# Memory heads of a two-block layer: the query and key weights multiplied into one matrix per head, and scores taken against the convolved rows

## The chip, the cores and the metric

The kernel runs on 1 core of one Trainium2 chip. The time is device microseconds of one execution. The kernel before takes 653.73 us, the median of 3 runs (653.63 to 653.75).

## The reference, cut to what matters

The program is two transformer blocks in a row on 256 rows of 1024 values, all in float32. The second block's mixer has eight attention heads and four memory heads (an mLSTM in chunks of 64, which the kernel computes over the whole 256 x 256 triangle). The memory heads take the rows `x_m`, convolve them over four positions, and form a query, a key and a value per head with 128 x 128 weights:

```
xc  = silu(_causal_conv(x_m, conv_w, conv_b))          # 256 x 512, four heads of 128
mq  = einsum('bshd,hde->bhse', xch, w_mq)
mk  = einsum('bshd,hde->bhse', xch, w_mk) * (128 ** -0.5)
mv  = einsum('bshd,hde->bhse', xmh, w_mv)
qk  = einsum('bhtd,bhsd->bhts', q_, k_) * w_intra       # scores, weighed by gates
...
ml_out = (hm + ml_skip * xc) * silu(z)
x = x + concatenate([attn_out, ml_out]) @ w_o
```

The key is used for nothing but the scores in this form. `xc` is used a second time, for the skip. After the mixer comes a mixture of experts (32 experts, two per row), whose weights (48 chunks of 2 MB) are read once, and a last gated projection.

## The kernel before, in words

Every engine has one instruction stream written out by hand, and counted semaphores order them. A semaphore's name with `_done` is raised by PE, one with `_ready` or `_high` mostly by ACT or DVE. Large products are split in a rounded and a remaining part (`product`, lines 2020 to 2022, three matmuls each).

The first block ends with `hand_over` on ACT (lines 771 to 794), which normalises the rows of each half of 128; PE meanwhile keeps busy with matmuls on zeros (`keep_busy`, L1996) and turns the rows with `turn_h` (L2015). Then, in the second mixer, PE makes in this order: the compressed projections (L2299), `x_m` and `z` (`tiles`), attention queries, keys and values (`product`), and then the stretch that the change touches. There `gate(0, ...)` makes the memory query (8 matmuls, L2397, of 256 columns, banks 2 and 3), three of six groups of attention scores come (L2413, with a mask matmul L2415), `gate(1, ...)` makes the memory key (8 more at L2397), three more groups of scores follow, two groups of transposed scores (L2459), and then a mix that is written out: `qk(h)` (the memory scores, L2432 and L2433, all in bank 6), `mix_values` (the memory values, L2467), `num(h)` (L2443 to L2445, all in bank 2), further transposed scores and `attend`. After them stand the products with `w_o`, without a break in PE's stream.

DVE in that stretch finds the maximum of each of the six score groups (L1651), then makes `round_wo(4)`, `round_wo(5)`, `weigh(0)`, `round_wo(6)`, `round_wo(7)`, `weigh(1)`, `divide(0)`, `weigh(2)` and so on. A `round_wo(n)` (L1660) copies an eighth of `w_o` (128 x 1024) to its rounded part, from SBUF to SBUF. A `weigh(h)` (L1667) multiplies the scores in bank 6 by the gates and so frees the bank for `qk(h + 1)`. A `divide(h)` frees bank 2 for `num(h + 1)`.

ACT copies the queries and keys out of PSUM (L1028 and L1053), makes the exponentials of the scores (L1040) and of the gates (L1046), and copies the values (L1060).

POOL makes `lower_wo(n)`, n = 0 to 7 (L712): the rest of each eighth of `w_o`, the raw weight less its rounded part, 128 x 1024, both inputs in SBUF. Its order is `lower_wo` 0 to 3, then a wait for `mk_done`, then the skip's two multiplications of `xcT` in place (L718, L720), then a wait until all eight parts are rounded, `lower_wo` 4 and 5, a multiplication of `szT` (L724), and `lower_wo` 6 and 7. Parts 0 to 3 are rounded by ACT early, 4 to 7 by DVE as above.

The DMA queue (SP) loads the weights in a fixed order. For the second mixer it issues `x_m`'s weights, `z`'s, `w_uq`, `w_ukv`, `w_mq`, `w_mk` and `w_mv` (L555 to L561), `w_o`'s halves, and then the experts' chunks into a ring of 12 places (`load_chunk`, L565). The first 12 are issued as places come free in the mixer; each later one waits until PE has used the chunk 12 before it. PE's loop over the experts holds a chunk until the last round of its group of four experts.

Of the kernel before, what the change touches and what calls it, by code (L numbers as in the profile page):

```python
# [22 lines left out]
P = 128  # L23
SEQ = 256
# [22 lines left out]
M_HEADS = 4  # L47
# [9 lines left out]
UNIT = 4096  # L57
# [12 lines left out]
def build(nc, a, out):  # L70
    with ExitStack() as ctx:
# [8 lines left out]
            "pe_mix2": (("c_done", 2), ("xm_done", 2), ("cT_done", 2), ("turned_done", 1), ("z2_done", 1),  # L80
                        ("gT_done", 1), ("negM_done", 1), ("z2_late", 1), ("negM_late", 1), ("qa_done", 4), ("ka_done", 4), ("v2_done", 2),
                        ("mq_done", 2), ("sa_done", 3), ("mk_done", 2), ("sa_late", 3), ("mv_done", 2)),
# [5 lines left out]
            "act_mix2": (("cs_ready", 1), ("cstd_ready", 1), ("gln_ready", 1), ("xm_ready", 2), ("ct_high", 1), ("lat_high", 3), ("sz_ready", 2),  # L88
                         ("xc_ready", 2), ("qn_ready", 2), ("xc_late", 2), ("qn_late", 2), ("kn_ready", 4), ("v2_ready", 2), ("mq_ready", 2),
                         ("floor_ready", 1), ("raw_ready", 3), ("wexp_ready", 1), ("mk_ready", 2), ("raw_late", 3), ("wexp_late", 3),  # L90
# [9 lines left out]
            "landed_root2": (("q1_landed", 16), ("wm_landed", 48)),  # L100
# [186 lines left out]
        mkT = v3(take(1024), 4)  # L287
# [153 lines left out]
        wm = W[:, 3 * UNIT:3 * UNIT + 1536].rearrange("p (m h e) -> p m h e", m=3, h=M_HEADS)  # L441
# [49 lines left out]
        def _(sp):  # L491
# [45 lines left out]
            sp.wait_ge(sig("x_ready"), 2)  # L537
            for dst, src in ((wr[:, :, 0:N_GRP], a["w_router_group_2"][0].rearrange("(k p) n -> p k n", p=P)),
                             (wr[:, :, N_GRP:36], a["w_router_expert_2"][0].rearrange("(k p) n -> p k n", p=P)),
                             (brt[:, 0:N_GRP], a["b_router_group_2"][0:1, :].broadcast_to([P, N_GRP])),  # L540
                             (brt[:, N_GRP:36], a["b_router_expert_2"][0:1, :].broadcast_to([P, N_EXP])),
                             (bif[:, 0:4], a["b_igate_2"][0:1, :].broadcast_to([P, M_HEADS])),
                             (bif[:, 4:8], a["b_fgate_2"][0:1, :].broadcast_to([P, M_HEADS])),
                             (pos.bitcast(I32), a["pos_tok"]),
                             (ptok, a["p_2"][0, 0].rearrange("(b p) c -> p b c", p=P))):
                sp.dma_start(dst, src).then_inc(sig("small_landed"), 16)
# [12 lines left out]
            sp.dma_start(wm[:, 0], a["w_mq_2"][0].rearrange("h d e -> d h e")).then_inc(sig("wm_landed"), 16)  # L559
            sp.dma_start(wm[:, 1], a["w_mk_2"][0].rearrange("h d e -> d h e")).then_inc(sig("wm_landed"), 16)  # L560
            sp.dma_start(wm[:, 2], a["w_mv_2"][0].rearrange("h d e -> d h e")).then_inc(sig("wm_landed"), 16)  # L561
# [68 lines left out]
        def _(pool):  # L630
# [84 lines left out]
            for n in range(4):  # L715
                lower_wo(n)
            pool.wait_ge(sig("mk_done"), at("mk_done", 2))
# [3 lines left out]
            pool.wait_ge(sig("dense_high"), 32 + 8 + 8)  # L721
            lower_wo(4)
            lower_wo(5)
# [24 lines left out]
        def _(act):  # L748
# [22 lines left out]
            def hand_over(r, b):  # L771

                n = 2 * r + b
                for h in range(2):
                    if h == 0:
                        act.wait_ge(sig("y_done"), n + 1)
                    else:
                        act.wait_ge(sig("yg_ready"), 2 * n + 1)
                    act.activation(junk[:, 512 * h:512 * h + 512], ps[:, 4 + 2 * b + h, :], ACT.Square, scale=D ** -0.5,
                                   accum_out=stat[:, 60 + h:61 + h]).then_inc(sig("ysq_ready"), 1)  # L780
                act.wait_ge(sig("yms_ready"), n + 1)
                act.wait_ge(sig("ysq_ready"), 2 * n + 2)
# [268 lines left out]
            for h in range(2):  # L1051
                act.wait_ge(sig("mk_done"), at("mk_done", h + 1))
                act.mul(mkT[:, 2 * h:2 * h + 2, :], v3(ps[:, 2 + h, :], 2), float(P) ** -0.5).then_inc(sig("mk_ready"), 1)  # L1053
# [937 lines left out]
        def _(pe):  # L1991
# [300 lines left out]
            keep_busy(0, 3)  # L2292
            turn_h(2, 0)
            keep_busy(3, 1)
            for b in range(TB):
                for k in range(KD):
                    if k % 4 == 0:
                        pe.wait_ge(sig("hT_ready"), 4 * 2 + 2 * b + k // 4 + 1)
                    last = pe.matmul(ps[:, 2 + b, 0:424], hT[:, k, b * P:(b + 1) * P], wA[:, k, :],  # L2299
                                     start=(k == 0), stop=(k == KD - 1))  # L2300
                    if b == 0 and k >= 6:
                        turn_h(2, 1, (k - 6,))
                last.then_inc(sig("c_done"), 1)
# [83 lines left out]
            pe.wait_ge(sig("wm_landed"), at("wm_landed", 48))  # L2387

            def gate(m, banks, name, free):

                for n in range(2):
                    for f in free[n]:
                        pe.wait_ge(sig(f[0]), at(*f))
                    pe.wait_ge(sig(("xc_ready", "xc_late")[n]), at(("xc_ready", "xc_late")[n], 2))
                    for i in range(2):
                        h = 2 * n + i
                        last = pe.matmul(ps[:, banks[n], 256 * i:256 * i + 256], wm[:, m, h, :], xcT[:, h, :], start=True, stop=True)  # L2397
                    last.then_inc(sig(name), 1)

            gate(0, (2, 3), "mq_done", ((("qn_late", 1), ("qr_late", 1)), (("qn_late", 2), ("qr_late", 2))))  # L2400
# [18 lines left out]
            for n in range(3):  # L2419
                scores(n)  # L2420
            gate(1, (2, 3), "mk_done", ((("mq_ready", 1),), (("mq_ready", 2),)))
            for n in range(3, 6):
                scores(n)

            def qk(h):

                if h == 0:
                    pe.wait_ge(sig("mq_ready"), at("mq_ready", 2))
                    pe.wait_ge(sig("mk_ready"), at("mk_ready", 2))
                else:  # L2430
# [16 lines left out]
            def turned_scores(n):  # L2447

                kb, h, heads = ST[n]
                o = v3(ps[:, ST_BANK[n], :], heads)  # L2450
                if n < 2:
                    pe.wait_ge(sig("mk_ready"), at("mk_ready", 2))
                elif n < 4:
                    pe.wait_ge(sig("raw_late"), at("raw_late", n))
                else:
                    pe.wait_ge(sig("e_ready"), at("e_ready", n - 3))
                for hh in range(heads):
                    for b in range(kb, TB):
                        last = pe.transpose(o[:, hh, (b - kb) * P:(b - kb + 1) * P], raw_block(b, h + hh, kb), ident[:])  # L2459
                last.then_inc(sig("st_done"), 1)  # L2460

            def mix_values():

                pe.wait_ge(sig("raw_late"), at("raw_late", 1))
                for b in range(TB):
                    for h in range(M_HEADS):
                        last = pe.matmul(ps[:, 4 + b, h * P:(h + 1) * P], xmT[:, h, 3 + b * P:3 + (b + 1) * P], wm[:, 2, h, :],  # L2467
                                         start=True, stop=True)
                    last.then_inc(sig("mv_done"), 1)
# [335 lines left out]
        "conv_ffn", "w_down", "p_2", "w_in_2", "w_ukv_2", "w_mq_2", "w_mk_2", "w_mv_2",  # L2805
# [39 lines left out]
```

## Time and profile before

| what | value |
|---|---|
| median of 3 runs | 653.73 us |
| the profiled execution, its own time | 653.55 us |
| its span | 651.8 us |
| granted clock, mean | 0.983 |
| PE / PEld busy | 616.8 us (95%) / 472.7 us (73%) |
| DVE / ACT / POOL busy | 378.9 us (58%) / 284.3 us (44%) / 47.7 us (7%) |
| read from HBM | 173.17 MB, 267 GB/s over the span |
| DMA traffic, 480 to 600 us | 423 to 432 GB/s |

Busy shares are means over stages with different limits. What counts for an edit is which wait ends last in its own stage. The stages that matter here are the second mixer (from 308 to 402 us), the routing (402 to 421.6 us), the experts (421.6 to 628 us) and the tail. Times within the span count from its start.

### The profile page before, as it was taken

How to read it: one execution, taken by the hardware profiler on the slowest of the kernel's cores; microseconds unless marked ns; L12 is line 12 of the kernel's file. 1: busy time of each engine (PE TensorE's matmuls, PEld its weight loads, DVE VectorE, ACT ScalarE, POOL GpSimd, SP SyncE). 2: the span in 40 equal slices, each digit the busy share in tenths (PEclk: the TensorE clock that was granted, in tenths of full speed). 3: DMA queues.
4: the chain of work that ended last, by engine and by line, in shares of the span. 5: the costliest groups of instructions: out<-in, count | busy, mean ns of one | idle time of the engine just before them, and what ended most of it. 6: DMA issues, size and time to landing. Idle time of an engine off the chain costs nothing. (4 is left out here: it accounts for less than half of the span.)

```text
span 651.8 us, 11050 instructions
## 1 busy us (share of the span) xinstructions
PE 616.8 (95%) x4314; PEld 472.7 (73%) x4318; DVE 378.9 (58%) x671; ACT 284.3 (44%) x454; POOL 47.7 (7%) x75
## 2 busy tenths in 40 slices
PE   8999999999999999999999999899999976769895
PEld 5999998899999999998699798644444431325365
DVE  5596868578777767766889475632222321103286
ACT  6773376575555555456794831610011000000184
POOL 3000000300000000001010860000000000000010
PEclk9999999999999999999999999999999997889998
DMA  8943543767755555500943698999899999999931
GB/s 328 371 161 130 179 130 113 272 190 257 233 189 177 179 177 176 187 3 2 379 153 130 259 350 309 429 426 427 343 427 430 426 423 429 429 425 425 424 165 66
DMA packets 52957, 174.82 MB, mean 268 GB/s; under 512 B 4790, under 2 KB 29490, under 8 KB 45874
## 3 DMA queue, kind: packets, MB, share of 16 engines
q1 hardware_dynamic: 52240, 172.54, 68.7%
q10 hardware_dynamic: 674, 1.69, 0.7%
q8 instruction: 30, 0.49, 0.3%
q14 instruction: 13, 0.11, 0.0%
HBM read 173.17 MB, written 1.05 MB: 267 GB/s over the span
## 5 line engine op out<-in xcount | busy, mean ns | idle before, releaser
L2020 PE MATMUL ps<-hT_high,w_up_parts 128*128 128x256 f32 x320 | 90.8, 284 | 0.0
L2022 PE MATMUL ps<-hT_high,w_up_parts 128*128 128x256 f32 x320 | 90.5, 283 | 0.0
L2021 PE MATMUL ps<-hT_low,w_up_parts 128*128 128x256 f32 x320 | 90.5, 283 | 0.0
L1423 DVE TENSOR_TENSOR w_up_parts<-W,w_up_parts 128x1024 fp32r<-128x1024 f32 x44 | 52.2, 1222 | 22.2 <-ACT w_up_parts L884 22.2
L2020 PEld LDWEIGHTS ps<-hT_high,w_up_parts 128*128 128x128 f32 x320 | 61.4, 192 | 0.5
L2021 PEld LDWEIGHTS ps<-hT_low,w_up_parts 128*128 128x128 f32 x320 | 61.4, 192 | 0.4
L2022 PEld LDWEIGHTS ps<-hT_high,w_up_parts 128*128 128x128 f32 x320 | 61.4, 192 | 0.0
L1104 ACT ACTIVATE sg<-ps 128x256 f32<-128x256 f32 x9 | 3.5, 384 | 123.0 <-PE ps L2633 123.0
L2633 PE MATMUL ps<-W,junk 128*32 128x512 f32 x368 | 45.7, 622 | 8.2 <-DMA W<-in_w_moe_dram 8.1
L884 ACT CAST w_up_parts<-W 128x1024 fp32r<-128x1024 f32 x44 | 44.5, 1048 | 20.3 <-PE ps L2022 19.0
L2020 PE MATMUL ps<-h_high,dense_high 128*128 128x256 f32 x160 | 45.8, 286 | 0.1
L2021 PE MATMUL ps<-h_low,dense_high 128*128 128x256 f32 x160 | 45.3, 283 | 0.0
L2022 PE MATMUL ps<-h_high,dense_low 128*128 128x256 f32 x160 | 45.3, 283 | 0.0
L1446 DVE SCALAR_TENSOR_TENSOR arena<-ps,arena 128x255 f32<-128x255 f32 x80 | 33.1, 476 | 17.2 <-ACT arena L920 16.9
L2617 PEld LDWEIGHTS ps<-arena,x_tok 128*128 128x128 f32 x288 | 32.8, 192 | 8.3 <-issue 6.7
L1297 DVE TENSOR_TENSOR dense_low<-W,dense_high 128x1024 fp32r<-128x1024 f32 x31 | 36.1, 1219 | 2.7 <-ACT dense_high L813 2.6
L2617 PE MATMUL ps<-arena,x_tok 128*128 128x128 f32 x288 | 34.4, 278 | 1.2 <-DVE arena L1878 1.2
L813 ACT CAST dense_high<-W 128x1024 fp32r<-128x1024 f32 x30 | 29.4, 1045 | 12.9 <-PE ps L2022 10.0
L2633 PEld LDWEIGHTS ps<-W,junk 128*32 128x32 f32 x368 | 10.5, 111 | 32.4 <-issue 19.8
L1871 DVE SCALAR_TENSOR_TENSOR sg<-sg,stat,ps 128x256 f32<-128x256 f32 x9 | 4.3, 481 | 48.1 <-ACT sg L1104 48.1
L2020 PE MATMUL ps<-w_down_high,uact_high 128*128 128x512 f32 x80 | 31.4, 392 | 0.1
L2020 PEld LDWEIGHTS ps<-h_high,dense_high 128*128 128x128 f32 x160 | 30.7, 192 | 1.0 <-issue 0.7
(500 smaller groups left out, 1386.5 us busy)
## 6 DMA issues: line engine op xcount, KB each, us to landing
W<-in_w_moe_dram SPq DMA_DIRECT2D x22, 2048.0 KB, 21.3
arena<-in_w_moe_dram SPq DMA_DIRECT2D x14, 2048.0 KB, 30.3
W<-in_w_up_dram SPq DMA_DIRECT2D x22, 1024.0 KB, 7.8
W<-in_w_in_dram SPq DMA_DIRECT2D x7, 2048.0 KB, 10.5
W<-in_w_down_dram SPq DMA_DIRECT2D x11, 1024.0 KB, 5.0
spare<-in_w_moe_dram SPq DMA_DIRECT2D x4, 2048.0 KB, 15.9
hh<-in_w_moe_dram SPq DMA_DIRECT2D x4, 2048.0 KB, 33.3
W<-in_w_out_dram SPq DMA_DIRECT2D x2, 2048.0 KB, 9.1
```

The source lines that it names most:

```text
L813: act.copy(piece(panel_hl(n)[0], n, c), piece(panel(n), n, c)).then_inc(sig("dense_high"), 1)
L884: act.copy(w_up_hl[0][:, c], U[q][:, :, g, i * P:(i + 1) * P]).then_inc(sig("up_high"), 1)
L1104: act.activation(sg, ps[:, 2, 0:F_EXP], ACT.Silu).then_inc(sig("sg_ready"), 1)
L1297: dve.tensor_tensor(piece(panel_hl(n)[1], n, c), piece(panel(n), n, c), piece(panel_hl(n)[0], n, c).bitcast(F32), ALU.subtract).then_inc(s ...
L1423: dve.tensor_tensor(w_up_hl[1][:, c], U[q][:, :, g, i * P:(i + 1) * P], w_up_hl[0][:, c].bitcast(F32), ALU.subtract).then_inc(sig("up_low" ...
L1446: dve.scalar_tensor_tensor(o, s, w, o, ALU.mult, ALU.add).then_inc(sig("tap_done"), 1)
L1871: dve.scalar_tensor_tensor(sg, sg, gslot, ps[:, 2, F_EXP:2 * F_EXP], ALU.mult, ALU.mult).then_inc(sig("a_ready"), 1)
L2020: pe.matmul(o, lhs[0], rhs[0], start=first, stop=False, skip_group_check=True)
L2021: pe.matmul(o, lhs[0], rhs[1], start=False, stop=False, skip_group_check=True)
L2022: return pe.matmul(o, lhs[1], rhs[0], start=False, stop=last_k, skip_group_check=True)
L2617: last = pe.matmul(ps[:, h, (k % 4) * P:(k % 4 + 1) * P], x_tok[:, b, k * P:(k + 1) * P], hot[:, b, :], start=(b == 0), stop=(b == 1))
L2633: last = pe.matmul(ps[CAP * c:CAP * c + CAP, 2, :], xg[:, k, CAP * c:CAP * c + CAP], up_chunk(CPG * g + j)[:, c, kk, :], start=(k == 0), s ...
```

## The change

In the hand-over between the blocks, PE multiplies each head's query weight by its key weight: `am[h] = w_mq[h] @ w_mk[h].T`, scaled by ACT. The former `gate(0)` uses `am` where it used `w_mq`; `gate(1)`, the key's copies on ACT and `mkT` go, and `qk` takes `xcT` where it took `mkT`. The two weights come in one transfer (512 KB, laid out by the host as transposes), issued early in the first block's MLP, in front of the small ones. Since `xcT` is now read by all four `qk`, POOL multiplies it in place only after the last of them, and makes `lower_wo` 4 and 5 ahead of that, each as soon as its own part is rounded.

```diff
 # SP
             sp.wait_ge(sig("x_ready"), 2)
+            sp.dma_start(wqk, a["w_mqk"]).then_inc(sig("wqk_landed"), 16)
             for dst, src in ((wr[:, :, 0:N_GRP], a["w_router_group_2"][0].rearrange("(k p) n -> p k n", p=P)),
...
-            sp.dma_start(wm[:, 0], a["w_mq_2"][0].rearrange("h d e -> d h e")).then_inc(sig("wm_landed"), 16)
-            sp.dma_start(wm[:, 1], a["w_mk_2"][0].rearrange("h d e -> d h e")).then_inc(sig("wm_landed"), 16)
-            sp.dma_start(wm[:, 2], a["w_mv_2"][0].rearrange("h d e -> d h e")).then_inc(sig("wm_landed"), 16)
+            sp.dma_start(wmv, a["w_mv_2"][0].rearrange("h d e -> d h e")).then_inc(sig("wm_landed"), 16)
 # POOL
-            for n in range(4):
+            for n in range(6):
                 lower_wo(n)
-            pool.wait_ge(sig("mk_done"), at("mk_done", 2))
+            pool.wait_ge(sig("qk_done"), 4)
             pool.tensor_tensor(xcT[:], xcT[:], szT[:], ALU.mult).then_inc(sig("gates_folded"), 1)
...
-            pool.wait_ge(sig("dense_high"), 32 + 8 + 8)
-            lower_wo(4)
-            lower_wo(5)
             pool.tensor_tensor(szT[:], szT[:], ...)
 # ACT, in hand_over, behind the two squares
+                if n == 3:
+                    act.wait_ge(sig("am_done"), at("am_done", 1))
+                    act.mul(am, v3(ps[:, 3, :], M_HEADS), float(P) ** -0.5).then_inc(sig("am_ready"), 1)
                 act.wait_ge(sig("yms_ready"), n + 1)
 # ACT, in the second mixer
             exp_gate(0)
-            for h in range(2):
-                act.wait_ge(sig("mk_done"), at("mk_done", h + 1))
-                act.mul(mkT[:, 2 * h:2 * h + 2, :], v3(ps[:, 2 + h, :], 2), float(P) ** -0.5).then_inc(sig("mk_ready"), 1)
 # PE, behind the first block
-            keep_busy(0, 3)
+            pe.wait_ge(sig("wqk_landed"), at("wqk_landed", 16))
+            for h in range(M_HEADS):
+                last = pe.matmul(ps[:, 3, h * P:(h + 1) * P], wqk[:, 0, h, :], wqk[:, 1, h, :], start=True, stop=True)
+            last.then_inc(sig("am_done"), 1)
             turn_h(2, 0)
-            keep_busy(3, 1)
+            keep_busy(2, 1)
...
+                    if b == 1 and k == 0:
+                        pe.wait_ge(sig("am_ready"), at("am_ready", 1))
 # PE, second mixer
-            for n in range(3):
-                scores(n)
-            gate(1, (2, 3), "mk_done", ((("mq_ready", 1),), (("mq_ready", 2),)))
-            for n in range(3, 6):
+            for n in range(6):
                 scores(n)
...
-                    pe.wait_ge(sig("mk_ready"), at("mk_ready", 2))
...
-                pe.matmul(ps[:, 6, 0:256], mkT[:, h, 0:P], mqT[:, h, :], start=True, stop=True)
-                pe.matmul(ps[:, 6, 256:384], mkT[:, h, P:SEQ], mqT[:, h, P:SEQ], start=True, stop=True).then_inc(sig("qk_done"), 1)
+                pe.matmul(ps[:, 6, 0:256], xcT[:, h, 0:P], mqT[:, h, :], start=True, stop=True)
+                pe.matmul(ps[:, 6, 256:384], xcT[:, h, P:SEQ], mqT[:, h, P:SEQ], start=True, stop=True).then_inc(sig("qk_done"), 1)
 # PE, turned_scores(n), n < 2
-                    pe.wait_ge(sig("mk_ready"), at("mk_ready", 2))
+                    pe.wait_ge(sig("raw_ready"), at("raw_ready", 2 + n))
```

## Rows read from the trace of the kernel before

**Rows 1.** The chain of waits that ended last: start us, us, what
```profile
421.59 0.54 issue
...
502.77 42.01 DMA W<-in_w_moe_dram
```

**Rows 2.** Busy time by engine in a stretch, around 460 us (stretch, its length, busy us and instructions, clock, DMA share, GB/s)
```profile
460.00:462.00 2.00, 2.00 (x22) 0.93 (x24) 1.39 (x3) 0.00 (x0) 0.00 (x0) 1.00 0.50 213
```

**Rows 3.** The DMA queue's issues in order of time
```profile
462.49 0.33 SPq L565 DMA_DIRECT2D W<-in_w_moe_dram  x1
```

**Rows 4.** Busy time by engine in a stretch of the second mixer
```profile
388.00:402.00 14.00, 14.00 (x71) 11.57 (x70) 10.78 (x33) 2.62 (x5) 0.32 (x1) 1.00 0.82 302
```

**Rows 5.** PE in order of time (start us, us, line, operation, count, idle before)
```profile
366.36 1.99 PE L2397 MATMUL ps<-arena,W 128*128 128x256 f32 x8
...
368.19 1.05 PE L2413 MATMUL ps<-arena 128*128 128x128 f32 x8
...
373.40 1.95 PE L2467 MATMUL ps<-W,arena 128*128 128x128 f32 x16
...
375.24 0.70 PE L2432 MATMUL ps<-arena 128*128 128x256 f32 x2
...
377.54 0.60 PE L2432 MATMUL ps<-arena 128*128 128x256 f32 x2
...
380.66 0.46 PE L2443 MATMUL ps<-arena,junk 128*128 128x129 f32 x2
```

**Rows 6.** ACT in order of time
```profile
310.95 0.29 ACT L783 ACTIVATE stat<-stat 128x1 f32<-128x1 f32 x1 [0.77 <-DVE stat L1247]
...
368.74 1.13 ACT L1053 ACTIVATE arena<-ps 128x512 f32<-128x512 f32 x2
...
370.21 1.14 ACT L1040 ACTIVATE W<-ps,arena 128x128 f32<-128x128 f32 x4 [0.34 <-DVE arena L1651]
```

**Rows 7.** ACT, DVE and PE early in the first block's MLP
```profile
143.58 3.90 ACT L884 CAST w_up_parts<-W 128x1024 fp32r<-128x1024 f32 x4 [0.97 <-DMA W<-in_w_up_dram]
...
158.27 0.69 DVE L1465 TENSOR_TENSOR uact_low<-arena,uact_high 128x512 fp32r<-128x512 f32 x1 [0.76 <-ACT uact_high L931]
...
160.87 0.40 PE L2020 MATMUL ps<-w_down_high,uact_high 128*128 128x512 f32 x1
```

**Rows 8.** POOL in order of time
```profile
369.02 2.35 POOL L718 TENSOR_TENSOR arena<-arena 128x1024 f32<-128x1024 f32 x1
...
371.45 1.89 POOL L720 TENSOR_TENSOR arena<-arena,par 128x1024 f32<-128x1024 f32 x1
...
376.69 2.36 POOL L712 TENSOR_TENSOR wo_low<-W,wo_high 128x1024 fp32r<-128x1024 f32 x1 [3.35 <-DVE wo_high L1660]
```

**Rows 9.** DVE in order of time, reductions, rounding copies and the weighing of scores
```profile
371.92 0.69 DVE L1651 TENSOR_REDUCE arena<-ps 128x2 f32<-128x512 f32 x1 [0.53 <-PE ps L2415]
...
372.65 1.24 DVE L1660 CAST wo_high<-W 128x1024 fp32r<-128x1024 f32 x1
...
375.10 0.69 DVE L1660 CAST wo_high<-W 128x1024 fp32r<-128x1024 f32 x1
...
375.10 1.51 DVE L1660 CAST wo_high<-W 128x1024 fp32r<-128x1024 f32 x2
...
376.52 0.55 DVE L1667 TENSOR_TENSOR junk<-ps,arena 128x384 f32<-128x384 f32 x1
```

**Rows 10.** POOL and DVE around 340 us
```profile
337.84 3.23 POOL L702 COPY arena<-arena 64x1792 f32<-64x1792 f32 x1 [28.96 <-DVE arena L1590]
...
338.32 1.20 DVE L1577 TENSOR_TENSOR z_low<-W,proj_high 128x1024 fp32r<-128x1024 f32 x1
...
339.45 2.15 DVE L1594 TENSOR_TENSOR_SCAN arena<-arena 4x256 f32<-4x256 f32 x1
...
342.09 0.68 DVE L1596 TENSOR_TENSOR_SCAN arena<-arena 4x256 f32<-4x256 f32 x1
```

**Rows 11.** DVE, its first instruction that needs the folded gates
```profile
397.23 0.69 DVE L1740 TENSOR_TENSOR hh<-ps,arena 128x512 f32<-128x512 f32 x1 [1.56 <-PE ps L2520]
```

More of the change, by code:

```diff
@@ L79, in build @@
                         ("o_done", 2), ("go_done", 2), ("onT_done", 2), ("u_done", 3), ("u_turned", 1)),
-            "pe_mix2": (("c_done", 2), ("xm_done", 2), ("cT_done", 2), ("turned_done", 1), ("z2_done", 1),
+            "pe_mix2": (("am_done", 1), ("c_done", 2), ("xm_done", 2), ("cT_done", 2), ("turned_done", 1), ("z2_done", 1),
                         ("gT_done", 1), ("negM_done", 1), ("z2_late", 1), ("negM_late", 1), ("qa_done", 4), ("ka_done", 4), ("v2_done", 2),
-                        ("mq_done", 2), ("sa_done", 3), ("mk_done", 2), ("sa_late", 3), ("mv_done", 2)),
+                        ("mq_done", 2), ("sa_done", 3), ("sa_late", 3), ("mv_done", 2)),
             "pe_route": (("oT_done", 2), ("hmT_done", 2), ("pT_done", 1), ("y2_done", 1), ("y2_half", 1), ("y2_late", 1), ("logits_done", 2), ("rank_done", 1),
@@ L87, in build @@
                          ("osq_ready", 1), ("ostd_ready", 1), ("sgo_ready", 2), ("uc_ready", 3)),
-            "act_mix2": (("cs_ready", 1), ("cstd_ready", 1), ("gln_ready", 1), ("xm_ready", 2), ("ct_high", 1), ("lat_high", 3), ("sz_ready", 2),
+            "act_mix2": (("am_ready", 1), ("cs_ready", 1), ("cstd_ready", 1), ("gln_ready", 1), ("xm_ready", 2), ("ct_high", 1), ("lat_high", 3), ("sz_ready", 2),
                          ("xc_ready", 2), ("qn_ready", 2), ("xc_late", 2), ("qn_late", 2), ("kn_ready", 4), ("v2_ready", 2), ("mq_ready", 2),
-                         ("floor_ready", 1), ("raw_ready", 3), ("wexp_ready", 1), ("mk_ready", 2), ("raw_late", 3), ("wexp_late", 3),
+                         ("floor_ready", 1), ("raw_ready", 3), ("wexp_ready", 1), ("raw_late", 3), ("wexp_late", 3),
                          ("mv_ready", 2), ("e_ready", 6), ("pT_ready", 1)),
@@ L99, in build @@
             "landed_root": (("q0_landed", 16), ("uq_landed", 32)),
-            "landed_root2": (("q1_landed", 16), ("wm_landed", 48)),
+            "landed_root2": (("q1_landed", 16), ("wqk_landed", 16), ("wm_landed", 16)),
             "pool_root": (("q_low", 1), ("krope_spread", 1)),
@@ L286, in build @@
         xmT = v3(take(4 * 259), 4)
-        mkT = v3(take(1024), 4)
+        off[0] += 512
+        am = v3(take(512), M_HEADS)
         vext = take(2 * 4 * 129).rearrange("p (b h e) -> p b h e", b=2, h=4)
@@ L439, in latent_piece @@
             return [t[:, :, 512 * j:512 * j + 512] for t in (uq, uq_hl[0], uq_hl[1])]
-        wm = W[:, 3 * UNIT:3 * UNIT + 1536].rearrange("p (m h e) -> p m h e", m=3, h=M_HEADS)
+        wmv = v3(W[:, 3 * UNIT + 1024:3 * UNIT + 1536], M_HEADS)
+        wqk = v4(spare[:, 0:1024], 2, M_HEADS)
         w_moe = a["w_moe"]
@@ L2386, in _ @@
                         [t.rearrange("p (h c) -> p h c", h=A_HEADS)[:, :, NOPE:P] for t in ukv_hl], True, True).then_inc(sig("v2_done"), 1)
[L2387 to L2400, printed above, removed]
+            for n in range(2):
+                pe.wait_ge(sig("qn_late"), at("qn_late", n + 1))
+                pe.wait_ge(sig("qr_late"), at("qr_late", n + 1))
+                pe.wait_ge(sig(("xc_ready", "xc_late")[n]), at(("xc_ready", "xc_late")[n], 2))
+                for i in range(2):
+                    h = 2 * n + i
+                    last = pe.matmul(ps[:, 2 + n, 256 * i:256 * i + 256], am[:, h, :], xcT[:, h, :], start=True, stop=True)
+                last.then_inc(sig("mq_done"), 1)
             pe.wait_ge(sig("v2_done"), at("v2_done", 2))
@@ L2466, in mix_values @@
                     for h in range(M_HEADS):
-                        last = pe.matmul(ps[:, 4 + b, h * P:(h + 1) * P], xmT[:, h, 3 + b * P:3 + (b + 1) * P], wm[:, 2, h, :],
+                        last = pe.matmul(ps[:, 4 + b, h * P:(h + 1) * P], xmT[:, h, 3 + b * P:3 + (b + 1) * P], wmv[:, h, :],
                                          start=True, stop=True)
@@ L2804 @@
 _INS = ["x", "norm_mix_post", "norm_ffn_post", "w_in", "gate_up_fwd", "gate_up_bwd", "w_out", "w_up",
-        "conv_ffn", "w_down", "p_2", "w_in_2", "w_ukv_2", "w_mq_2", "w_mk_2", "w_mv_2",
+        "conv_ffn", "w_down", "p_2", "w_in_2", "w_ukv_2", "w_mv_2",
         "b_igate_2", "b_fgate_2", "w_o_2", "w_router_group_2", "b_router_group_2", "w_router_expert_2",
@@ L2834 @@
     laid_out["w_q"] = _np.asarray(inputs["w_in"])[0][:, C_Q:C_Q + 512].reshape(KD, P, 4, P).transpose(1, 2, 0, 3).reshape(P, UNIT)
+    laid_out["w_mqk"] = _np.stack([_np.asarray(inputs[name])[0].transpose(2, 0, 1) for name in ("w_mq_2", "w_mk_2")], axis=1)
     laid_out["w_gate"] = _np.asarray(inputs["w_ple_gate_2"])[0].reshape(KD, P, 2, 512).transpose(2, 1, 0, 3)
```

## The prediction

> **What bounds the kernel now.** I read the chain that ended last first. From 502.77 us it runs on DMA: an expert chunk is issued when PE frees its place and lands 42.01 us later, behind all the others in the queue [rows 1]. Before that the chain is PE's own, back to 421.59 us, where PE enters the loop over the experts. Next I read the windows around 460 us, to see whether the DMA engines or PE set the moment at which that backlog begins. They do not move anything for half of the stretch from 460 to 462 us (share 0.50) [rows 2], because the queue's next issue stands at 462.49 us, behind a chunk that PE holds through the second round of its group [rows 3]. So DMA has run dry for about 1.5 us, and it starts again a fixed distance behind PE's start at 421.59. Whatever moves that start moves the end by the same amount, up to about 1.5 us of slack the other way if only DMA were early; since the earlier loads hang on the same PE steps, they move along.
>
> What sets 421.59? The windows of the second mixer show PE busy for all 14.00 us from 388 to 402 [rows 4], and the rows ahead of it follow each other without a gap: the key's matmuls run from 366.36 for 1.99 us, and the next score has begun at 368.19 [rows 5]. PE's stream has no cover there: an instruction taken out of it, or a wait put into it, counts in full, unless another engine is late next.
>
> **What is taken out.** The memory key's eight matmuls start at 366.36 and the next score starts at 368.19 [rows 5]: 8 instructions, 1.83 us. ACT loses two copies of PSUM, 1.13 us together [rows 6]. That one is worth nothing by itself, because right behind it ACT waited 0.34 us for DVE's maximum of group 3, which hangs on PE's scores [rows 6]; all of that moves with PE. With nothing else the sum is -1.83 us.
>
> **What is put in, and costs nothing or nearly.** Four 128-column matmuls stand where three on zeros stood, in a stretch where PE only waits for the normalised rows. By `mix_values`, sixteen of the same shape in 1.95 us [rows 5], they take 0.12 each, 0.49 together; the price is between 0 (the zeros took as long) and 0.5; I take 0. ACT's scaling of `am` is one 128 x 512 copy out of PSUM, 0.57 us by the pair at L1053 [rows 6]. It falls where ACT stood idle for 0.77 us before L783 [rows 6]: hidden with 0.2 us to spare; without that cover it would cost up to 0.6. The third new wait (`am_ready`, at PE's second compressed projection) comes microseconds after the copy. `qk` has the same shapes with `xcT` as with `mkT`: 0. The transposed scores now wait for `raw_ready`, which ACT reaches before 368.74 (its next rows [rows 6]), while PE gets there only behind the last maximum's scores, which end just ahead of 371.92 - 1.83 = 370.1 [rows 9]: 0.
>
> The 512 KB transfer goes into the queue early in the first MLP, ahead of eight small ones and of the loads of `w_up`. Those are exposed a little: ACT waited 0.97 us for one at 143.58 [rows 7]. 512 KB at 427 GB/s (the middle of the table's 423 to 432) are 1.2 us. ACT's and DVE's chain then reaches `uact_low` at 158.96 + 1.2 = 160.2 us instead of 158.96 (the row at 158.27, 0.69 long), and PE asks for it at 160.87 [rows 7]: hidden, with 0.7 us left. Bounds: 0, and up to 1.7 us if the queue takes 3.6 us over it. `w_mq` and `w_mk` leaving the later queue helps nobody who waits: 0.
>
> **What is moved: POOL.** This is where I see the change give back its gain. Before, DVE's four rounding copies run at 372.65 and after. POOL's subtractions of the same parts, L712, begin at 376.69, behind the last copy [rows 8]: the two never overlap. Only the first copy meets POOL, which works on L720 until 371.45 + 1.89 = 373.34 [rows 8]. That copy takes 1.24 us, while the one at 375.10 takes 0.69 with POOL idle [rows 9]. 1.24 is exactly 0.69 (from 372.65 to 373.34) plus 0.55. So either DVE stood still until POOL was through, or it ran at nearly half speed throughout. The scan at 339.45 decides for standing still, as far as one row can: 2.15 us against 0.68 for the same shape at 342.09, and it ends at 341.60, which is 0.53 behind the end of POOL's copy (337.84 + 3.23 = 341.07) [rows 10]. The maxima, which read PSUM, are not touched (0.69 for the maximum at 371.92, beside POOL's L720) [rows 8, 9].
>
> The Trainium skill says the same more sharply: "SBUF — State Buffer", section "Who interferes with whom", gives DVE and GpSimd one shared pair of ports, which whoever issues first holds for its whole instruction, and names copies and casts within SBUF among the DVE instructions that need it. By that rule the sum below is +0.8 to +1.3 us; by a mere slowing of the copies it is -1.1.
>
> After the change POOL makes `lower_wo(4)` as soon as copy 4 is done, and `lower_wo(5)` as soon as copy 5 is, right among DVE's copies 5, 6 and 7. Step by step, with DVE's last maximum at 371.92 - 1.83 = 370.09 and the copy 0.73 behind it as now [rows 9]:
> - copy 4: 370.82 to 371.51 (POOL idle). POOL starts 0.08 later, at 371.59 (now it starts at 376.69, and the two copies from 375.10 end 1.51 later, at 376.61), and takes 2.36 [rows 8, 9]: to 373.95.
> - copy 5 is stopped until 373.95 and ends 0.55 later, 374.50. `weigh(0)` to 375.0. PE has been ready for `qk(1)` since 375.24 - 1.83 = 373.41 [rows 5] and waits 1.6 us.
> - POOL's second subtraction runs from 374.58 to 376.94. Copy 6 is stopped and ends at 377.49; copy 7 ends at 378.30; `weigh(1)` runs to 378.78.
> - PE starts `qk(2)` at 378.8. Before it started at 377.54 [rows 5]: +1.3 us instead of -1.83.
>
> What follows is a chain between PE and DVE (`num`, `divide`, `weigh`) whose next link, `num(2)` at 380.66 [rows 5], moves along by as much, and behind it PE's stream is full. If DVE gets in first with copy 5 (it asks 0.13 us behind its copy 4, by 1.51 less twice 0.69 [rows 9]; POOL 0.08), that copy is free, but POOL's two subtractions still stand in front of copies 6 and 7. Then the order is 371.64 to 372.33, POOL to 374.6, copy 6 to 375.1, POOL to 377.3, copy 7 to 377.8, `weigh(1)` to 378.3: +0.8 us. If POOL needs the ports only after some start-up, both its blocks shrink; with 0.5 us less in each the sum is about +0.1. I take +0.9 us, near the middle of the two full orders.
>
> POOL's later work costs nothing. It begins behind `qk(3)`, near 382 (3.2 us behind the new `qk(2)`), and holds 2.35 + 1.89 us for `xcT`, another 1.89 for `szT` (the same shape) and twice 2.36 for the last two parts [rows 8]: it ends near 393. DVE asks for the folded gates at 397.23 [rows 11], PE for the last parts of `w_o` later still.
>
> **The sum.** Against the profiled execution (span 651.8 and 1.75 around it, 653.55 us, 0.18 below the median of the runs): 653.55 - 1.83 + 2.73 = 654.45. On the median of the runs: 653.73 + 0.9 = 654.6 us.
>
> **The rivals.**
> - *DVE slips its last copy in.* If copy 7 comes to the ports before POOL's second subtraction, only one block of POOL counts. `weigh(1)` then ends near 376.0 and `qk(2)` starts at 376.05: -1.5 us, 652.2. For it: the gaps of 0.08 and 0.13 us are so close that the order is open; and DVE's L1577, issued 0.48 us behind POOL's copy at 337.84, was not held up (1.20 us) [rows 10]. Against it: POOL's instruction is already waiting when DVE asks. Chance 0.13.
> - *Copies slowed, not stopped.* Copies 5 to 7 take 1.24 us each. `weigh(1)` ends at 376.35 and `qk(2)` starts at 376.4: -1.1 us, 652.6. For it: 1.24 us fits this too. Against it: the scan. Chance 0.15.
> - *No collision that counts; the full gain.* -1.83 us, 651.9. It needs DVE and POOL not to meet at all, against the row at 372.65 [rows 9]. Chance 0.10.
> - *Slower by the early transfer.* If issuing the 512 KB delays the next `w_up` load by more than 1.9 us (160.87 less 158.96) [rows 7], PE waits in the first MLP. At 3.6 us that is +1.7 on top of the forecast: 656.3. It decides from 1.9 us on. Against it: 512 KB are only 1.2 us of transfer, and the later parts of the MLP let ACT catch up. Chance 0.07.
> - The change does do what it says in the scores: PE loses the eight matmuls in any case.
>
> **How the numbers follow.** The forecast (the two engines in turn, +0.1 to +1.3) has 0.55. From no change this kernel's runs can be told at about 0.2%, 1.3 us. The forecast lies mostly inside that and reaches its edge in its worst order, so of its 0.55 I give 0.35 to no change and 0.20 to slower. The first rival is faster (0.13), the second almost all no change (0.11, and 0.04 faster), the third faster (0.10), the fourth slower (0.05) or no change (0.02). Together: faster 0.27, same 0.48, slower 0.25. The range goes from 652.0, which takes in the first two rivals and nearly the third, to 655.3, just above the worst order; about 0.15 is left out. The likeliest case alone spans 653.8 to 655.1.
>
> **What the profile after would show.** Right: copies 5 to 7 at L1660's new line longer than 0.69, at least two of them about 2 us or more, ending 0.55 behind POOL's ends; `weigh(1)` near 378; PE idle for 1 to 3 us in front of `qk(1)` and `qk(2)`, released by DVE; the expert loop starting near 422.5. Wrong: `qk(2)` at 376.5 or earlier, or copies of 1.24 (the second rival). Also wrong would be an ACT row `am` that pushes L783 past 310.95, a wait of PE in the first MLP near 160 us, or a different number of rounds per expert group, since rounding differs and a row near a tie could choose another expert.

## The result, and the profile after

The kernel after takes 656.70 us, the median of 5 runs (656.38 to 656.92), beside 653.63 us for five runs of the kernel before (653.12 to 653.75). The ratio of the two is 1.0046, with a 95% interval of 1.0035 to 1.0058: slower by about 3.1 us, where +0.9 was forecast. Its profiled execution took 656.92 us with a span of 655.2 (before 651.8), 3.4 us more. The rest of this section finds these 3.4.

The chain of waits that ended last (start, length, what) still goes through PE's entry into the loop over the experts:

```profile
424.99 0.51 issue
```

It stood at 421.59 [rows 1], so it comes 3.40 later, which is the whole difference of the spans. Everything was lost ahead of it. The instructions of both traces, matched in order, differ by a constant except at the places that follow, in order of time.

**The first MLP.** PE's first matmuls start up to 0.24 us later here; in the other kernels of this study this offset was between -0.1 and +0.25, so it is read as a scatter of the start. ACT's wait for a load of `w_up`, and the rest of that chain on DVE and PE (ACT, DVE and PE in order of time, each with its start, length and idle time before):

```profile
145.33 1.05 ACT L885 CAST w_up_parts<-W 128x1024 fp32r<-128x1024 f32 x1 [2.45 <-DMA W<-in_w_up_dram]
```

```profile
160.02 0.69 DVE L1463 TENSOR_TENSOR uact_low<-arena,uact_high 128x512 fp32r<-128x512 f32 x1 [0.76 <-ACT uact_high L932]
```

```profile
161.11 0.40 PE L2018 MATMUL ps<-w_down_high,uact_high 128*128 128x512 f32 x1
```

The load makes ACT 1.75 us later (2.45 us idle where it was 0.97 [rows 7]) and ends DVE's instruction at 160.71. PE reaches the product at 161.11, the 0.24 later with which it started: 0.40 us of cover were left, of which 0.24 come from PE's own late start.

**The hand-over.** PE in order of time, then ACT:

```profile
308.70 1.13 PE L2292 MATMUL ps<-spare 128*128 128x128 f32 x8 [0.30 <-PE ps L2020]
309.67 1.04 PE L2013 MATMUL ps<-ident,hh 128*128 128x128 f32 x8
```

```profile
310.34 0.59 ACT L781 ACTIVATE arena<-ps 128x512 f32<-128x512 f32 x1
311.69 0.30 ACT L784 ACTIVATE stat<-stat 128x1 f32<-128x1 f32 x1 [0.75 <-DVE stat L1245]
```

The product of the weights, L2292, holds PE for 0.97 us, from 308.70 to 309.67, and is 8 rows of the trace though the code has four matmuls. The turn of the rows behind it starts 0.74 later than before (309.67 for 308.93). Of the 0.50 that are new, about two thirds are the product, and a third is there without it too (the run with the transfer alone, below). ACT's L784, which was L783 and stood at 310.95 [rows 6], is late by the same 0.74 (0.24 of the start and 0.50 new). ACT's own scaling of `am`, L781, costs nothing: ACT is idle for 0.75 us behind it.

**The missing key.** The first score of the mixer is late by 0.73 us, and the fourth group starts early:

```profile
367.08 1.16 PE L2410 MATMUL ps<-arena 128*128 128x128 f32 x8
...
371.75 0.60 PE L2425 MATMUL ps<-arena 128*128 128x256 f32 x2
```

Before, the same scores stood at 368.19 [rows 5] and the first `qk` here:

```profile
372.75 0.60 PE L2432 MATMUL ps<-arena 128*128 128x256 f32 x2
```

That is -1.00 at the `qk`, and -1.74 from one side of the removed matmuls to the other. (The first row of the scores alone is 1.11 earlier, the rows behind it 1.00.)

**DVE and POOL.** DVE in order of time; copies 4 and 5 are shown together as x2, then copy 5 by itself, and copies 6 and 7 each by itself:

```profile
371.65 1.52 DVE L1658 CAST wo_high<-W 128x1024 fp32r<-128x1024 f32 x2
...
372.48 0.69 DVE L1658 CAST wo_high<-W 128x1024 fp32r<-128x1024 f32 x1
...
373.09 0.55 DVE L1665 TENSOR_TENSOR junk<-ps,arena 128x384 f32<-128x384 f32 x1
373.55 2.39 DVE L1658 CAST wo_high<-W 128x1024 fp32r<-128x1024 f32 x1
...
376.08 2.62 DVE L1658 CAST wo_high<-W 128x1024 fp32r<-128x1024 f32 x1
...
378.62 0.55 DVE L1665 TENSOR_TENSOR junk<-ps,arena 128x384 f32<-128x384 f32 x1
```

POOL's two subtractions over the same stretch, together and the first alone:

```profile
372.49 5.66 POOL L713 TENSOR_TENSOR wo_low<-W,wo_high 128x1024 fp32r<-128x1024 f32 x2 [2.81 <-DVE wo_high L1658]
```

```profile
372.49 2.91 POOL L713 TENSOR_TENSOR wo_low<-W,wo_high 128x1024 fp32r<-128x1024 f32 x1 [2.81 <-DVE wo_high L1658]
```

Copies 4 and 5 (the x2 from 371.65) are free, 0.69 each. POOL is released behind copy 4 at 372.49 and stands still for copy 5, which begins at 372.48: its instruction takes 2.91 instead of 2.36 [rows 8] and ends at 375.40. Copy 6 is asked for at 373.55 and ends at 375.94, 0.54 behind that. Copy 7 ends at 378.70, 0.56 behind POOL's second end (372.49 + 5.66 = 378.15). `weigh(1)` ends at 379.17, and PE waits for it. PE in order of time:

```profile
376.17 0.27 PE L2452 MATMUL ps<-ident,W 128*128 128x128 f32 x1
376.28 0.27 PE L2452 MATMUL ps<-ident,arena 128*128 128x128 f32 x1
379.22 1.22 PE L2425 MATMUL ps<-arena 128*128 128x256 f32 x2 [2.66 <-DVE junk L1665]
...
380.66 0.42 PE L2452 MATMUL ps<-ident,W 128*128 128x128 f32 x1
380.87 0.42 PE L2452 MATMUL ps<-ident,arena 128*128 128x128 f32 x1
...
383.17 0.60 PE L2425 MATMUL ps<-arena 128*128 128x256 f32 x2
```

`qk(2)` starts at 379.22, where it started at 377.54 [rows 5]: the shift, -1.00 at the first `qk` and -1.15 just ahead of the wait, has gone to +1.68. This wait of 2.66 us is the one wait for DVE that PE has between 372 and 388 us.

**The clock.** In the same rows `qk(2)` takes 1.22 us for two rows of 256 columns, while the next `qk` at 383.17 takes 0.60 for the same. Busy time by engine in stretches (stretch, length, PE, PEld, DVE, ACT, POOL, granted clock, DMA share, GB/s):

```profile
378.00:380.00 2.00, 0.78 (x2) 0.69 (x3) 1.90 (x6) 0.00 (x0) 0.14 (x1) 0.81 1.03 378
380.00:382.00 2.00, 2.00 (x11) 1.91 (x10) 0.64 (x2) 0.25 (x1) 0.00 (x0) 0.50 0.87 367
382.00:384.00 2.00, 1.99 (x13) 1.75 (x12) 0.91 (x4) 0.95 (x3) 0.00 (x0) 0.84 0.00 0
372.00:388.00 16.00, 13.23 (x95) 12.52 (x94) 12.20 (x27) 7.57 (x15) 9.36 (x4) 0.89 0.68 238
```

and of the kernel before, for the last of these:

```profile
372.00:388.00 16.00, 15.90 (x133) 15.45 (x133) 12.34 (x35) 9.14 (x18) 12.34 (x6) 1.00 0.76 285
```

Behind the wait the granted clock is 0.50, the lower of TensorE's two levels (1.2 instead of 2.4 GHz), for about 3.4 us: a mean of 0.81 over 2 us is 0.76 us at half clock, then come 2.00, and 0.84 is 0.64. Rows of 128 columns follow each other at 0.21 us (380.66 and 380.87) where they did at 0.11 (376.17 and 376.28), and the shift grows row by row from +1.68 to +3.44. From there to 424.99 it changes by no more than 0.04.

So the balance of the profile is +0.24 (start), +0.50 (hand-over: the product of the weights and PE's wait in front of it), -1.74 (key), +2.68 (wait for DVE, from -1.00 to +1.68), +1.76 (half clock): 3.44 us, of which 3.40 are left at 424.99.

### The profile page after: what moved, and what is told of

It is laid out like the page before. It is cut to its first block and busy times, and to the rows that moved or that the text cites. A ratio compares the mean times of both kernels' runs of the same rounds, so it can differ in the third digit from the quotient of the medians.

```text
span 655.2 us, 11044 instructions
## 1 busy us (share of the span) xinstructions
PE 617.4 (94%) x4315; PEld 473.9 (72%) x4315; DVE 382.0 (58%) x671; ACT 283.5 (43%) x453; POOL 48.7 (7%) x75
```

## The experiments

Theory A: the loss is the collision of POOL's two early subtractions with DVE's copies, and the clock that falls behind the wait which it makes. Rival B: the collision only, and the clock would have fallen somewhere anyway. Rival C: the loss comes from the transfer in the first MLP. Rival D: from the new product in the hand-over. The runs of the first four kernels stand beside 18 runs of the kernel before (median 653.39 us), those of the last four beside 28 (653.59). Each ratio is that of a kernel's median to these.

**POOL's two parts behind all copies again, all else as after.**

```diff
-            for n in range(6):
+            for n in range(4):
                 lower_wo(n)
+            pool.wait_ge(sig("dense_high"), 32 + 8 + 8)
+            lower_wo(4)
+            lower_wo(5)
             pool.wait_ge(sig("qk_done"), 4)
```

> The changed kernel with one edit undone: POOL again waits until all eight parts of w_o are rounded before it makes the rest of parts 4 and 5 (the fold of xcT stays behind the last qk). Theory (POOL and DVE stop each other, PE then stands idle for 2.7 us, and its clock falls for 3.4 us): DVE's four copies take 0.69 us each, PE does not wait in front of the third qk, the clock stays at 1.0 through the second mixer, and the whole loss of that stretch goes: about 4.5 us less than the changed kernel's 656.7, so 652.2 to 652.7. Rival (POOL's order is harmless, the loss comes from the weights' product, the early transfer and the qk that now reads xcT): 656 to 657, PE still waiting.

Measured: 652.13 us (651.63 to 653.23, 10 runs), ratio 0.9982 (0.9972 to 0.9991). DVE, POOL and PE in order of time:

```profile
371.46 1.52 DVE L1661 CAST wo_high<-W 128x1024 fp32r<-128x1024 f32 x2
...
373.37 1.51 DVE L1661 CAST wo_high<-W 128x1024 fp32r<-128x1024 f32 x2
```

```profile
375.01 4.80 POOL L713 TENSOR_TENSOR wo_low<-W,wo_high 128x1024 fp32r<-128x1024 f32 x2 [5.55 <-DVE wo_high L1661]
```

```profile
376.20 0.60 PE L2428 MATMUL ps<-arena 128*128 128x256 f32 x2
```

```profile
372.00:388.00 16.00, 15.89 (x130) 15.32 (x129) 11.95 (x38) 7.96 (x16) 12.68 (x6) 1.00 0.86 328
```

All four copies are free, `qk(2)` waits for nothing and starts 1.34 us earlier than before, and the clock stays at 1.00 from 372 to 388 us (the last row). Moving two instructions of POOL turned 3.1 us slower into 1.3 us faster. Rivals C and D are out as main causes, since both edits are still in this kernel.

**Zeros into PE's wait.** The collision is left alone; twelve matmuls on zeros stand in front of `qk(2)`.

```diff
             turned_scores(3)
+            keep_busy(4, 12)
             qk(2)
```

> The changed kernel with 12 matmuls on zeros (bank 4, free by then) put in front of the third qk, where PE stands idle for 2.7 us; they take about 2.6 us at full clock. Theory (the idle stretch makes the clock fall, and that costs 1.8 us by itself): qk still starts near 379.2, held by DVE, but the clock stays at 1.0 and the time is 1.7 us less, 655.0. Rival (the clock falls there for another reason, or work on zeros does not hold it): half clock again and 656.7. Rival 2 (zeros delay the qk): above 656.7.

Measured: 655.04 us (654.50 to 656.84, 5 runs), ratio 1.0034 (1.0020 to 1.0048). PE, DVE and the windows:

```profile
376.28 2.54 PE L1994 MATMUL ps<-zb 128*128 128x512 bf16 x11
378.91 0.70 PE L2425 MATMUL ps<-arena 128*128 128x256 f32 x2
```

```profile
373.23 5.16 DVE L1658 CAST wo_high<-W 128x1024 fp32r<-128x1024 f32 x2
378.31 0.55 DVE L1665 TENSOR_TENSOR junk<-ps,arena 128x384 f32<-128x384 f32 x1
```

```profile
378.00:380.00 2.00, 1.91 (x12) 1.24 (x11) 1.80 (x7) 0.00 (x0) 0.00 (x0) 1.00 1.05 406
380.00:382.00 2.00, 2.00 (x17) 1.78 (x15) 1.33 (x5) 1.17 (x2) 0.00 (x0) 1.00 0.63 263
```

Eleven of the twelve matmuls on zeros are in the trace. The copies are stopped as in the kernel after (5.16 us for two), `qk(2)` starts as late as in the kernel after (0.31 earlier), but the clock is 1.00 where it was 0.50. From `qk(2)` to the expert loop it now takes 423.02 - 378.91 = 44.11 us, against 424.99 - 379.22 = 45.77: the fall of the clock is worth 1.66 us in the profile. Rival B is out for this place. In the medians the difference is 1.4 us if each is set against its own runs of before (+3.07 and +1.65), but the two intervals of the ratios overlap, and the profiled execution is the fastest of its five. So the profile settles that the clock stays up, while what its fall costs in the medians is known only roughly.

**POOL's order alone, on the kernel before.** Only `lower_wo(4)` and `(5)` are moved ahead of the folding; the key, the queue and the hand-over stay.

```diff
-            for n in range(4):
+            for n in range(6):
                 lower_wo(n)
             pool.wait_ge(sig("mk_done"), at("mk_done", 2))
...
-            pool.wait_ge(sig("dense_high"), 32 + 8 + 8)
-            lower_wo(4)
-            lower_wo(5)
```

> The kernel before with POOL's order changed alone: it makes the rest of parts 4 and 5 right behind their roundings, ahead of the fold of xcT; keys, weights and transfers are as before. Theory (each block of 2.35 us stops a copy of DVE until it is through, then the clock falls): copies 6 and 7 near 2.4 us each, the third qk near 380.2 instead of 377.5 (+2.7), and +1.7 more for the half clock: 657.5 to 658.2. With stopping but no fall of the clock: 656.3. Rival (copies only slowed to 1.24 us each): at most +1, 654.5. Rival (POOL's order is harmless): 653.6.

Measured: 657.50 us (656.03 to 657.65, 4 runs), ratio 1.0056 (1.0039 to 1.0073). PE, DVE, and the windows in the wait and behind it:

```profile
380.26 0.72 PE L2429 MATMUL ps<-arena 128*128 128x256 f32 x2 [2.67 <-DVE junk L1664]
```

```profile
374.59 2.40 DVE L1657 CAST wo_high<-W 128x1024 fp32r<-128x1024 f32 x1
...
377.12 2.62 DVE L1657 CAST wo_high<-W 128x1024 fp32r<-128x1024 f32 x1
```

```profile
378.00:380.00 2.00, 0.00 (x0) 0.00 (x0) 2.00 (x2) 0.21 (x1) 1.92 (x2) 1.00 1.02 367
380.00:382.00 2.00, 1.74 (x8) 1.69 (x9) 1.57 (x6) 0.00 (x0) 1.95 (x1) 0.70 1.02 378
382.00:384.00 2.00, 2.00 (x12) 2.00 (x11) 0.34 (x4) 0.58 (x1) 1.98 (x2) 0.50 0.43 180
```

The same two blocked copies, the same wait (2.67) and the same half clock, without any other part of the change: the expert loop starts at 425.72, 4.13 late. The clock is not down while PE stands still: it is 1.00 from 378 to 380 us, where PE does nothing, and the mean of 0.70 in the next 2 us is 1.2 us at half clock, so it fell near 380.8, half a microsecond after PE was back at 380.26. In the kernel after, the same sum puts the fall near 379.24, and PE was back at 379.22. This edit by itself costs more than the whole change; the rest of the change gives back 0.7 of it (4.13 against 3.40), mostly the key less the hand-over.

**The product of the weights in two halves**, one in front of the turn of the rows and one behind it, where zeros stood.

```diff
-            for h in range(M_HEADS):
-                last = pe.matmul(ps[:, 3, h * P:(h + 1) * P], wqk[:, 0, h, :], wqk[:, 1, h, :], start=True, stop=True)
-            last.then_inc(sig("am_done"), 1)
+            def weight_product(h):
+
+                return pe.matmul(ps[:, 3, h * P:(h + 1) * P], wqk[:, 0, h, :], wqk[:, 1, h, :], start=True, stop=True)
+
+            weight_product(0)
+            weight_product(1)
             turn_h(2, 0)
-            keep_busy(2, 1)
+            weight_product(2)
+            weight_product(3).then_inc(sig("am_done"), 1)
```

> The changed kernel with the weights' product of two heads in front of the first turn of the rows and of two heads behind it (and without the one matmul on zeros there). Theory (a 128-column float32 matmul is two records of 0.11 us, so that the four take 0.97 us in front of the turn, where only 0.5 has cover, and all that follows is 0.5 us late): turn back by about 0.5 us, and 656.3 in all, 0.3 to 0.5 less than the changed kernel. Rival (the 0.5 us there come from ACT's scaling of the product): no gain, 656.7 or more, since ACT gets the product later.

Measured: 655.89 us (654.16 to 657.50, 8 runs), ratio 1.0032 (1.0017 to 1.0048). PE and ACT at the hand-over:

```profile
308.56 0.68 PE L2293 MATMUL ps<-spare 128*128 128x128 f32 x4 [0.30 <-PE ps L2020]
309.07 1.04 PE L2013 MATMUL ps<-ident,hh 128*128 128x128 f32 x8
309.95 0.61 PE L2293 MATMUL ps<-spare 128*128 128x128 f32 x4
```

```profile
311.10 0.29 ACT L784 ACTIVATE stat<-stat 128x1 f32<-128x1 f32 x1
```

ACT's L784 goes from 311.69 to 311.10, 0.59 earlier, and matched instructions show 0.50 of it as the product's (0.09 is the start). So rival D is worth half a microsecond in the profile, no more. The eight runs scatter over 3.3 us, more than those of any other kernel here. The profiled one has the full wait (2.67) and the half clock; whether the three runs between 654.16 and 654.41 escaped the fall is not shown by any trace and stays open. Their mean clocks would allow it: 0.986 to 0.988, beside 0.979 to 0.983 in the five slower runs, where 3.4 us at half clock are worth 0.003; but the runs of the kernel before, without a fall at this place in its profile, range from 0.981 to 0.990 as well.

**One part early, one late.**

```diff
-            for n in range(6):
+            for n in range(5):
                 lower_wo(n)
+            pool.wait_ge(sig("dense_high"), 32 + 8 + 8)
+            lower_wo(5)
             pool.wait_ge(sig("qk_done"), 4)
```

> The changed kernel, but POOL makes only the rest of part 4 early; that of part 5 waits until all eight parts are rounded. Theory (each POOL instruction holds DVE's next copy once, and the clock falls only behind a long idle stretch of PE): copy 6 takes 2.4 us, copy 7 0.7; the third qk waits 0.8 us instead of 2.7, and the clock stays at 1.0: about 1.0 us above the kernel with both late (652.1), 653.1. Rival (any idle stretch there makes the clock fall): half clock and about 654.8. Rival (one early part is free): 652.1.

Measured: 653.26 us (652.65 to 654.91, 10 runs), ratio 0.9995 (0.9986 to 1.0004).

```profile
377.29 0.70 PE L2427 MATMUL ps<-arena 128*128 128x256 f32 x2 [0.74 <-DVE junk L1667]
```

```profile
372.00:388.00 16.00, 15.16 (x126) 14.54 (x125) 12.59 (x34) 8.15 (x16) 12.56 (x6) 1.00 0.85 327
```

One blocked copy (2.39 us) leaves PE a wait of 0.74 us, and the clock does not fall: 1.00 from 372 to 388 us. The step from this kernel to the kernel after, one more blocked copy, is 1.9 us of wait and 1.6 us of clock (45.77 less 44.15 in the table below).

**The same two parts early, each as two instructions of 512 columns.**

```diff
-                pool.tensor_tensor(wo_low[h][o], PAN[4 + h][o], wo_part(h, q)..., ALU.subtract)...
+                if n in (4, 5):
+                    k = 2 * q
+                    pool.tensor_tensor(wo_low[h][:, k, :], PAN[4 + h][:, k, :], wo_part(h, q)[:, 0, :]..., ALU.subtract).then_inc(sig("rest_half_done"), 1)
+                    pool.wait_ge(sig("rest_half_done"), n - 3)
+                    pool.tensor_tensor(wo_low[h][:, k + 1, :], PAN[4 + h][:, k + 1, :], wo_part(h, q)[:, 1, :]..., ALU.subtract)...
+                else:
...
```

> The changed kernel with POOL's order as it is, but the rests of parts 4 and 5 made in two instructions each (128 x 512 instead of 128 x 1024), so that POOL gives the ports back twice as often. Theory (a copy waits for the POOL instruction in hand, not for POOL's work): copies 6 and 7 wait for one half each, 1.2 to 1.7 us instead of 2.4 and 2.6, the third qk waits 0.3 to 0.8 us, the clock stays up: 652.5 to 653.2. Rival (it is the sum of POOL's work in that stretch that counts): copies and time as in the changed kernel, 656.7.

Measured: 653.01 us (652.74 to 653.72, 10 runs), ratio 0.9991 (0.9982 to 1.0001). DVE, then PE:

```profile
373.28 1.31 DVE L1664 CAST wo_high<-W 128x1024 fp32r<-128x1024 f32 x1
...
374.72 1.55 DVE L1664 CAST wo_high<-W 128x1024 fp32r<-128x1024 f32 x1
```

```profile
376.79 0.70 PE L2431 MATMUL ps<-arena 128*128 128x256 f32 x2 [0.51 <-DVE junk L1671]
```

POOL does the same work at the same place, but a copy waits only for the instruction in hand: 1.31 and 1.55 instead of 2.39 and 2.62. POOL's four instructions follow each other at gaps of 0.07 to 0.08 us here. A mere slowing of DVE while POOL works would have left the copies as long as they were, so this decides for standing still. POOL stands still in its turn: the first three of its instructions take 1.82, 1.61 and 1.59 us, and the fourth, which meets no copy, 1.27.

**The transfer alone, on the kernel before.** The 512 KB are loaded where the change loads them and used by nothing.

```diff
             sp.wait_ge(sig("x_ready"), 2)
+            sp.dma_start(wqk, a["w_mqk"]).then_inc(sig("wqk_landed"), 16)
...
             pe.wait_ge(sig("a2_landed"), 16)
+            pe.wait_ge(sig("wqk_landed"), 16)
```

> The kernel before with the 512 KB transfer of the query and key weights added in its new place (PE waits for it behind the first block; the weights aren't used). Theory (it delays the next load of w_up by 1.2 to 1.8 us, which ACT and DVE make good within two pairs of tiles): ACT's wait for that load at 143.6 us grows from 1.0 to about 2.5, PE waits at most 0.2 us, the time is 653.4, as before. Rival (it is on the path): 654.9 or more.

Measured: 653.90 us (653.51 to 655.64, 10 runs), ratio 1.0009 (1.0000 to 1.0018). ACT and DVE:

```profile
145.35 3.90 ACT L886 CAST w_up_parts<-W 128x1024 fp32r<-128x1024 f32 x4 [2.80 <-DMA W<-in_w_up_dram]
```

```profile
160.04 0.69 DVE L1467 TENSOR_TENSOR uact_low<-arena,uact_high 128x512 fp32r<-128x512 f32 x1 [0.76 <-ACT uact_high L933]
```

ACT is 1.77 us late and has made it good when the trace is at 178 us, but the cover was all but used up: DVE's instruction ends at 160.73 and PE begins the product at 160.79, and PE's rows around it go from 0.06 ahead of before to 0.03 to 0.07 behind. At the hand-over PE is 0.16 later still, presumably by the wait for the weights, the one thing that is new there; its three matmuls on zeros take 0.65 us there (308.52 to 309.17), which the product of the weights, at 0.97, exceeds by 0.32. The expert loop starts at 421.78 (+0.19), and the span is unchanged, 651.8. The medians differ by 0.3 us and the interval of the ratio allows up to 1.2, so rival C can't be the 3.1.

**Both repairs**: POOL's order of the first experiment and the halves of the fourth, nothing else.

> The changed kernel with both repairs: POOL's rests of parts 4 and 5 behind all eight roundings, and the weights' product in halves around the first turn of the rows. Theory: the gain of the missing eight key matmuls is kept, 1.75 us, and nothing else is lost: 651.5 to 651.8, about 0.5 below the first repair alone (652.1). Rival (the halves only move the delay to ACT): 652.1 or more.

Measured: 651.53 us (651.17 to 651.86, 6 runs), ratio 0.9969 (0.9957 to 0.9981). This beats both kernels, by 2.1 us against before, and lies in the expected range. From the first repair alone (652.13) it differs by 0.6 us, less than the scatter of that kernel's runs; in the profiles `qk(2)` comes 0.64 earlier, of which about 0.2 is the start. PE's `qk(2)` and the chain's entry into the expert loop:

```profile
375.56 0.60 PE L2432 MATMUL ps<-arena 128*128 128x256 f32 x2
```

```profile
419.59 0.51 issue
```

The kernels beside each other, from their profiles, with the last column worked out:

| kernel | `qk(2)` starts | PE's wait before it | expert loop starts | between | clock fell |
|---|---|---|---|---|---|
| before | 377.54 | 0 | 421.59 | 44.05 | no |
| POOL late | 376.20 | 0 | 420.22 | 44.02 | no |
| both repairs | 375.56 | 0 | 419.59 | 44.03 | no |
| short blocks | 376.79 | 0.51 | 420.91 | 44.12 | no |
| one early | 377.29 | 0.74 | 421.44 | 44.15 | no |
| zeros | 378.91 | filled | 423.02 | 44.11 | no |
| after | 379.22 | 2.66 | 424.99 | 45.77 | yes |
| product in halves | 378.62 | 2.67 | 424.34 | 45.72 | yes |
| POOL's order alone | 380.26 | 2.67 | 425.72 | 45.46 | yes |

The last distance takes one of two values: 44.02 to 44.15 where the clock stood, 45.46 to 45.77 where it fell, and in this stretch it fell behind the long waits alone.

## Why the prediction was wrong

The direction of the forecast was right (+0.9), the size was not (+3.1), and the time lies above the range's end of 655.3.

- *What moves PE's entry into the expert loop moves the end:* right. Over all kernels the spans follow the loop's start within 0.6 us, except for the kernel with one part early (+1.4 beside -0.15), whose profiled execution was also its slowest of ten; where it lost the rest is open.
- *The key's matmuls, -1.83:* -1.74 measured.
- *The two engines in turn, an issued instruction holding the other back:* right, to the place and nearly to the number. The order was the second that the step named (DVE first with copy 5, then POOL in front of copies 6 and 7). It put `weigh(1)` at 378.3; with the stretch in front of it 0.83 less early than the text took it (-1.00 instead of -1.83) that is 379.1, measured 379.17. The gain of 1.74 and the wait give +0.9 by themselves, which is the forecast. The Trainium skill's "SBUF — State Buffer", section "Who interferes with whom", gives DVE and GpSimd one pair of ports as an exclusive lock; 2.39 and 2.62 us against 0.69, and 1.31 and 1.55 behind half as long an instruction, agree.
- *The step that failed:* the chain behind `qk(2)`. The text let PE wait for 1 to 3 us, said that the next link "moves along by as much, and behind it PE's stream is full", and priced the rest at nothing. A stream that is full runs at the clock that is granted, and behind 2.66 us without a matmul the clock was at half for about 3.4 us: +1.76 in the profile, 1.66 by the experiment with zeros. The sum had no term for it, and no rival named it, though the prediction itself listed the idle time among what the profile after would show.
- *The term mis-sized:* the hand-over, the product of the weights taken at 0 with 0.5 as its upper bound. `mix_values` has sixteen rows in 1.95 us [rows 5], but its loop has eight matmuls (two halves, four heads): an fp32 matmul of this kind leaves two rows. Four of them are 0.97 us, not 0.49; the three matmuls on zeros that they replace are 0.65, so about 0.33 came through. The other 0.16 or so of the measured 0.50 are presumably PE's new wait: the run with the transfer alone has it too, and is 0.16 late there without the product. The sum had no term for it. That 0.50 is just the bound is chance: with 0.49 for the product the zeros would have covered all of it. The same miscount called the key's four matmuls eight (and the query's, in the description of the kernel), harmlessly, because there the time was read off the starts.
- *ACT's scaling, the transfer in the first MLP, POOL's late folding:* right that they cost nothing or nearly. But the transfer delayed ACT by 1.75 us, not by the 1.2 taken: only 0.15 short of the 1.9 from which it was to cost time, where the text saw 0.7 left. PE's own late start of 0.24 helped; with the transfer alone PE lost about 0.1 us there. POOL was through at 395.2, and DVE asked for the folded gates at 400.66.
- *The rivals:* the copy slipped in front of POOL's second part, the slowing and the full gain did not happen. These three lost on their mechanism: copies 6 and 7 stood behind POOL in every trace that had both parts early. The fourth, the early transfer, lost by the 0.15 us just named.

The two missing terms, 0.50 and 1.76, are 2.26 us; with +0.9 that makes 3.2, beside the measured +3.07. What the start's 0.24 us is remains within the scatter of the runs.

## What to carry to other kernels

Before an instruction of POOL is moved next to DVE's copies within SBUF, put both in order of time and let each wait for the whole instruction of the other; where they must meet, cut POOL's instructions in two. Where a sum lets PE stand still for microseconds, add a term for the clock behind it, and weigh filling the wait with matmuls on zeros. And count matmuls in the code, not in the trace's rows, before a time per row becomes a price.

## What the runs showed of the hardware that was not expected

- A wait of PE of 2.66 or 2.67 us was followed by the half clock in all three profiles that have one; waits of 0.51 and 0.74 us in the same place were not. Nothing between was tried. The fall came with PE's return in one (379.24 and 379.22) and about half a microsecond after it in another (380.8 and 380.26); within the wait the clock was still 1.00.
- Matmuls on zeros in the wait kept the clock at 1.00, although they produce nothing that is used.
- An instruction of POOL that the trace starts 0.01 us behind a copy of DVE (372.49 and 372.48) did not get its turn first: it took 2.91 us instead of 2.36, though POOL had been released by the copy before.
- A blocked copy ended 0.54 to 0.56 us behind POOL's end in each case, not 0.69, as if 0.14 us of a copy were already past when POOL ends. What this part is, was not measured.
